# Dissolving the table stage of a decoder step into the gather stage that follows it

## What is computed

```
score = einsum(relu(qi . ki), wi)                 # cheap scores over all keys
_, idx = top_k(score, 256)                        # per sample: 256 of 4097 keys
k_sel, v_sel = cache[page_table[idx // 128], idx % 128]
logits = q . k_sel / 8 + rel_bias[t5_bucket(qpos - idx)]
p = softmax(where(valid, logits, -inf));  o = p . v_sel
merged = sigmoid(gate_a) * (att @ w_attn_out) + sigmoid(gate_s) * (ssd_y @ w_ssd_out)
```

## Time and profile before

| what | value |
| --- | --- |
| median of 3 runs | 4491.07 us (4490.77 to 4492.65) |
| the profiled execution | 4487.59 us |
| its span | 4485.8 us |
| PE, DVE, ACT, POOL busy | 91%, 41%, 16%, 5% of the span |
| mean granted clock of PE | 0.942 of full speed |
| table stage | 2677.1 to 2706.5 us of the span |
| gather stage | 2706.5 to 2879.1 us of the span |

### The profile page before, as it was taken

The page is one execution under the profiler, slowest core; times in us unless marked ns, Lnnn a source line. Parts: engine busy times, 40 slices in busy tenths (PEclk is TensorE's granted clock), DMA queues, the critical chain, the costliest instruction groups (busy, mean ns, idle before and its releaser), DMA issues. The chain is left out here.

```text
span 4485.8 us, 48370 instructions
## 1 busy us (share of the span) xinstructions
PE 4092.7 (91%) x17960; PEld 2927.2 (65%) x17960; DVE 1838.2 (41%) x3624; ACT 725.8 (16%) x1421; POOL 223.2 (5%) x224
## 2 busy tenths in 40 slices
PE   7999999989977978988988978899988989999997
PEld 5888776656655555665655645566656678888664
DVE  4222220010035676586586575257861143333001
ACT  2000000010021220211311300145611010000000
POOL 0000000000000020010100201200000100000000
PEclk9999999999957989999999988899998999999999
DMA  4121221114132101101001011320022111111111
GB/s 171 76 112 76 94 96 64 45 70 169 71 78 64 36 22 57 38 16 57 33 21 57 28 32 56 100 71 19 6 82 96 65 50 47 38 47 42 69 39 57
DMA packets 98898, 277.21 MB, mean 62 GB/s; under 512 B 18473, under 2 KB 54321, under 8 KB 87073
## 3 DMA queue, kind: packets, MB, share of 16 engines
q1 hardware_dynamic: 80464, 239.13, 15.5%
q0 software_dynamic: 3200, 21.11, 1.3%
q10 hardware_dynamic: 15072, 14.82, 1.1%
HBM read 228.18 MB, written 47.00 MB: 61 GB/s over the span
## 5 line engine op out<-in xcount | busy, mean ns | idle before, releaser
L1648 PE MATMUL banks<-h,arena 128*128 128x344 f32 x1920 | 586.6, 465 | 30.9 <-DMA arena<-in_w_ssd 30.9
L472 PE MATMUL f_ps<-f_a,f_w 128*128 128x344 f32 x2112 | 611.2, 452 | 1.9 <-issue 1.9
L472 PEld LDWEIGHTS f_ps<-f_a,f_w 128*128 128x128 f32 x2112 | 401.1, 190 | 211.3 <-issue 2.3
L1648 PEld LDWEIGHTS banks<-h,arena 128*128 128x128 f32 x1920 | 368.7, 195 | 232.9 <-DMA arena<-in_w_ssd 32.7
L363 PE MATMUL f_ps<-h,f_w 128*128 128x258 f32 x1408 | 327.7, 386 | 13.0 <-ACT h L209 12.1
L363 PE MATMUL f_ps<-room 128*128 128x258 f32 x1408 | 328.3, 393 | 2.5 <-issue 1.8
L363 PE MATMUL f_ps<-h,room 128*128 128x258 f32 x1408 | 320.9, 381 | 1.1 <-DVE f_u L633 1.0
L363 PEld LDWEIGHTS f_ps<-h,f_w 128*128 128x128 f32 x1408 | 269.7, 192 | 64.5 <-issue 23.6
L363 PEld LDWEIGHTS f_ps<-room 128*128 128x128 f32 x1408 | 275.1, 196 | 45.8 <-issue 2.7
L363 PEld LDWEIGHTS f_ps<-h,room 128*128 128x128 f32 x1408 | 266.9, 190 | 41.0 <-DVE f_u L633 1.9
L707 PE MATMUL banks<-y,arena 128*128 128x344 f32 x768 | 239.2, 474 | 38.2 <-DVE y L2058 30.1
(11 more groups left out here) (380 smaller groups left out, 4866.4 us busy)
## 6 DMA issues: line engine op xcount, KB each, us to landing
f_wa<-in_w_ada SPq DMA_DIRECT2D x28, 1024.0 KB
f_w<-in_w_f1i SPq DMA_DIRECT2D x22, 1024.0 KB, 4.7
f_w<-in_w_f2i SPq DMA_DIRECT2D x22, 1024.0 KB, 4.7
arena<-in_w_ssd SPq DMA_DIRECT2D x40, 512.0 KB, 3.6
f_w<-in_w_f1o SPq DMA_DIRECT2D x16, 704.0 KB, 4.1
f_w<-in_w_f2o SPq DMA_DIRECT2D x16, 704.0 KB, 4.1
room<-in_x SPq DMA_DIRECT2D x16, 516.0 KB, 7.7
scr_x<-room SPq DMA_DIRECT2D x16, 516.0 KB, 5.2
```

The costliest lines, as they stand in the source:

```text
L472: m = nc.tensor.matmul(ps[n][:, q, 0:NC], wo[:, hf, k], a[:, hf * OK + k, n * NC:(n + 1) * NC], start=hf == 0 and k == 0, stop=hf == 1 and ...
L1648: m = nc.tensor.matmul(ps[q][:, c, 0:NC], w[:, q, k], h[:, k, c * NC:(c + 1) * NC], start=k == 0, stop=k == KT - 1)
```

## The change

`tables` is removed as a stage, and its work is written into the streams of `gate_and_gather`:

- SP issues the three table loads first, then the first two gate tiles; then it waits for the subtraction, stores the tables, waits for the stores, issues the read-back, and goes on with the gate tiles (written out instead of looped). The table's buffers are cut out of `kvb`, which the gathers fill later.
- PE makes the table products first, into the banks of the later one-hot products. The three chunks of the first gate tile are set between the selection's products, and the eight flips between the second and the third gate tile, with a wait for the read-back ahead of them and a wait for all eight copies behind them. The loop is written out.
- DVE handles the table products ahead of the selection, and copies the flips between the mask's scaling and the first one-hots.
- POOL waits ahead of its first gather until the flips are done and the bias rows stored; its last wait, for the landed rows, is dropped. DVE waits for them before it reads the keys in `sample_attend_and_out`, PE before it reads the values. The index buffers therefore live on past the stage (`rows_at`).

```diff
-def tables(nc, d, s, bias):
-    ...
 def gate_and_gather(...)
+        at, up = carve(kvb, 0, [P, NH, WIN])
+        at, hot = carve(kvb, at, [NBUCKET, 512])
...
+        pf = [pE[n // 2][n % 2] for n in range(4)]
...
         def _(sp):
-            load_tiles(sp, w, w_in, gmm, NCH, d["w_gs"], KT)
+            sp.dma_start(hot, d["hot"]).then_inc(tabled, 16)
+            sp.dma_start(rb, d["rel_bias"]).then_inc(tabled, 16)
+            sp.dma_start(flip, d["flip"]).then_inc(tabled, 16)
+            for t in range(KT):
+                if t == 2:
+                    sp.wait_ge(sub, UP + 1)
+                    sp.dma_start(scr["byh"], byh).then_inc(b_stored, 16)
+                    sp.dma_start(scr["brow"].rearrange("(c p) h -> p c h", c=2), brow_t).then_inc(b_stored, 16)
+                    sp.wait_ge(b_stored, UP + 32)
+                    win = bass.AP(scr["byh"].tensor, 0, [[1, P], [512, NH], [1, WIN]])
+                    sp.dma_start(up, win).then_inc(b_back, 16)
+                if t >= 2:
+                    sp.wait_ge(gmm, UP + NCH * (t - 1))
+                sp.dma_start(w[:, t % 2], d["w_gs"][t]).then_inc(w_in[t % 2], 16)
...
         def _(pe):
+            pe.wait_ge(tabled, UP + 48)
+            nc.tensor.matmul(pf[0][0:NH, :], rb, hot, start=True, stop=True).then_inc(tabbed, 1)
+            for c in range(2):
+                nc.tensor.matmul(pf[1][:, c * NH:(c + 1) * NH], hot[:, c * P:(c + 1) * P], rb, ...).then_inc(tabbed, 1)
             pe.wait_ge(split, UP + 4)
...
+            chunk(0, 0)
             pe.wait_ge(chosen, UP + 1)
...
+            chunk(0, 1)
             pe.wait_ge(ranked, UP + 1)
...
-            gate(0, 0)
-            gate(0, 1)
+            chunk(0, 2)
+            gate(1)
+            pe.wait_ge(b_back, UP + 16)
+            pe.wait_ge(sub, UP + 1)
+            for n in range(NH // 2):
+                if n >= 4:
+                    pe.wait_ge(flipped, UP + n - 3)
+                nc.tensor.matmul(pf[n % 4][:], flip, up[:, 2 * n:2 * n + 2]...).then_inc(tabbed, 1)
             pe.wait_ge(valsd, UP + 1)
-            with pe.Fori(0, NB // 4) as i:
+            pe.wait_ge(flipped, UP + NH // 2)
+            for j in range(NB // 2):
+                gate(BEFORE + j)
...
         def _(dve):
+            dve.wait_ge(tabbed, UP + 3)
+            nc.vector.tensor_copy(byh, pf[0][0:NH, :]).then_inc(moved, 1)
+            nc.vector.tensor_copy(brow_t, pf[1][:, 0:2 * NH]...).then_inc(moved, 1)
+            dve.wait_ge(moved, UP + 2)
+            nc.vector.tensor_scalar(byh, byh, pf[0][0:NH, 0:1], None, ALU.subtract).then_inc(sub, 1)
...
+            for n in range(NH // 2):
+                dve.wait_ge(tabbed, UP + 4 + n)
+                nc.vector.tensor_copy(bias[:, 2 * n:2 * n + 2]..., pf[n % 4][:]).then_inc(flipped, 1)
...
         def _(pool):
+            pool.wait_ge(flipped, UP + NH // 2)
+            pool.wait_ge(b_stored, UP + 32)
...
-            pool.wait_ge(gathered, n)
...
 def sample_attend_and_out(...)
...
             pe.wait_ge(ptd, UP + 1)
+            pe.wait_ge(gathered, GATHERED)
...
             take(1)
+            dve.wait_ge(gathered, GATHERED)
```

More of the change, by code:

```diff
@@ L2128, in ssd_branch, with gate_and_gather @@
             ssd_out(nc, arena, banks, d, g, xc, zs, y, ones, dskip, nssd, S, mask)
-def gate_and_gather(nc, d, scr, h, S, mask, ident, pick, gathered, cnt, seln, kvb, brows, spare):
+def gate_and_gather(nc, d, scr, h, S, mask, ident, pick, gathered, cnt, seln, kvb, brows, rows_at, spare, bias):
     RING = 2 * NPAGE
@@ L2150, in gate_and_gather @@
         where = ph.sb("where", [P, 3, NB, 2])
-        row = ph.sb("row", [P, NB, 2], U32)
-        brow = ph.sb("brow", [P, NB, 2], U32)
+        row, brow = rows_at[:, 0], rows_at[:, 1]
+        at, up = carve(kvb, 0, [P, NH, WIN])
+        at, hot = carve(kvb, at, [NBUCKET, 512])
+        at, rb = carve(kvb, at, [NBUCKET, NH])
+        at, byh = carve(kvb, at, [NH, 512])
+        at, brow_t = carve(kvb, at, [P, 2, NH])
+        at, flip = carve(kvb, at, [P, P])
+        tabled, tabbed, moved, sub, b_stored, b_back, flipped = (
+            ph.sem(n) for n in ("tabled", "tabbed", "moved", "sub", "b_stored", "b_back", "flipped"))
         kv = kv_view(kvb)
@@ L2196, in _, with chunk, gate @@
         def _(pe):
-            def gate(i, q):
-                pe.wait_ge(w_in[q], UP + 16 * (i + 1))
-                for c in range(NCH):
[L2200 to L2205, removed]
+            def chunk(t, c):
+                q = t % 2
+                if c == 0:
+                    pe.wait_ge(w_in[q], UP + 16 * (t // 2 + 1))
+                if t:
+                    pe.wait_ge(gread, UP + NCH * (t - 1) + c + 1)
+                for k in range(KT):
+                    m = nc.tensor.matmul(ps[:, c, 0:NC], w[:, q, k], h[:, k, c * NC:(c + 1) * NC], start=k == 0, stop=k == KT - 1)
+                m.then_inc(gmm, 1)
+            def gate(t):
+                for c in range(NCH):
+                    chunk(t, c)
+            pe.wait_ge(tabled, UP + 48)
+            nc.tensor.matmul(pf[0][0:NH, :], rb, hot, start=True, stop=True).then_inc(tabbed, 1)
+            for c in range(2):
+                nc.tensor.matmul(pf[1][:, c * NH:(c + 1) * NH], hot[:, c * P:(c + 1) * P], rb, start=True, stop=True).then_inc(tabbed, 1)
             pe.wait_ge(split, UP + 4)
@@ L2602, in program @@
             kvb = buf(c2, "kvb", [P, 2 * (PAST + 1)])
[L2603 removed]
+            brows, rows_at = buf(c2, "brows", [P, NB, 2, NH]), buf(c2, "rows_at", [P, 2, NB, 2], U32)
             kT, qs = buf(c2, "kT", [P, 2, TOK]), buf(c2, "qs", [P, NH // 2, NB])
@@ L2606, in program @@
                 bias = buf(c3, "bias", [P, NH, WIN])
-                tables(nc, d, scr, bias)
-                gate_and_gather(nc, d, scr, h, S, mask, ident, pick, gathered, cnt, seln, kvb, brows, kT)
+                gate_and_gather(nc, d, scr, h, S, mask, ident, pick, gathered, cnt, seln, kvb, brows, rows_at, kT, bias)
                 attend(nc, d, scr, h, kT, qs, tok, mask, bias, ident, att)
-            sample_attend_and_out(nc, d, scr, kT, qs, tok, ones, ident, cnt, seln, kvb, brows, att, h, mask)
+            sample_attend_and_out(nc, d, scr, gathered, kT, qs, tok, ones, ident, cnt, seln, kvb, brows, att, h, mask)
         sums = buf(ctx, "sums", [P, 3, TOK])
```

32 lines of the change are left out of this document (17 added, 15 removed).

## The result

| | before | after |
| --- | --- | --- |
| median (4 runs each) | 4491.55 us (4490.77 to 4492.65) | 4447.11 us (4440.19 to 4451.94) |
| ratio, 95% interval | | 0.99 [0.9883, 0.9917] |
| profiled execution, its span | 4487.59, 4485.8 us | 4440.19, 4438.0 us |
| first table load to the load of kT for the prompt's attention | 201.95 us | 158.66 us |

What follows compares the result with a forecast made beforehand. TensorE bounds the gather stage once gate products run, with a chain of waits ahead. Saving 16.6 us there, minus 0.8 for stage ends, plus 0.4 for loops, gives 16.2: 4491.1 to 4474.9 us, range 4470 to 4483.

Steps and rivals of the forecast that it cites:

- The sum to the third gate tile: From the first table load's issue to the third gate tile: 50.8 us against 67.4, 16.6 us less.
- Table loads: Start of the stage: loads now share the queues with other loads and weight tiles, +1.0 us on their 2.82.
- Store and read-back, selection: Ahead of the third gate tile: 11.82 us of store and read-back, waits of 2.46 and 1.73, hidden under gate products.
- Flips: After the second gate tile: 9.0 us against 9.29 before, with two TensorE gaps of some 1.3 and 0.85 us.
- Clock at the flips: TensorE's gaps at the flips cost no clock: 0 charged, 1.7 us as the other bound.
- The clock rival: Clock falls at the small products between chunks, transposes and flips: 5.1 to 8.7 us, 4480.0 to 4483.6; chance 0.15.
- late loads: Table loads land late and hold the selection: 3.5 us more than charged, 4478.4; chance 0.10 together with uncovered selection.
- a late read-back: TensorE waits before the flips for the 2 MB read-back; slower if over 9 us, time then 4500; chance 0.04.
- an uncovered selection: Gate chunks fail to cover the selection's waits: 4.2 us come back, 4479.1; chance 0.10 together with late loads.
- Stage ends: The table stage's seven semaphores are now cleared at the gather stage's end: 0.8 us charged, bounds 0 and 1.0.
- Unrolled loops: TensorE's gate loop written out saves the 0.44 us gap at its turn: 0.4 credited, bounds -0.5 and 0.5.
- something unseen: Remainder for causes not listed anywhere in the forecast: chance 0.05, about half of it slower.

Runs made afterwards that it cites:

- loop_const_addr: Kernel before, TensorE's loop kept, but both turns read the first four samples' page and row numbers, so one-hot product addresses are constant: 4473.5 us, ratio 0.9961.
- register_addr: Changed kernel, gate tiles still written out, one-hot products in loops of two turns with a register in their address: 4472.79 us, ratio 0.9965.
- loop_ends_only: Changed kernel with a loop of one turn round each half group of one-hot products, all addresses constant: 4446.34 us, ratio 0.9901 to before.
- attention_written_out: Changed kernel with TensorE's loops in the prompt's attention written out too: 4447.43 us, ratio 0.9905 to before.
- mask_later: Changed kernel with VectorE's scaling of the mask moved behind the flips' copies: 4445.33 us, ratio 0.9903 to before.
- written_out_mask_later: Changed kernel with TensorE's prompt attention loops written out and the mask's scaling behind the flips' copies: 4453.16 us, ratio 0.9918 to before.

## Why the prediction was wrong

The table part was right, by its own steps.

- *The sum to the third gate tile*: 50.8, measured 50.31; selection's first product at t = 9.52, under the 12 that I set. That it is this close is partly luck: the loads (+0.2), the spread products (+0.3) and the flips (+0.4: 9.38 us from 2716.27 to 2725.65) took longer, the gate tiles (-0.5) and the two selection products between them (-0.7) less.
- *Table loads*: TensorE starts 4.02 us after the first issue (2679.36 - 2675.34), 1.2 more than before; I charged 1.0.
- *Store and read-back, selection*: both hidden. Without the chunks 5.8 us come back, where I had 4.2: the loads came 0.6 later in that run, and the lone products took 0.59 and 0.69 us, not 0.28 and 0.38; that is 1.2 of the 1.6 us between.
- *Flips*: two gaps, 1.25 and 0.83 (forecast 1.3 and 0.85); the eighth copy ends some 9 us after the second gate tile.
- *Clock at the flips*: 1.00 over the whole stretch (2716.20:2725.60 above). The Trainium skill's rule ("TensorE: Matmul & The Clock Gate", "A second HAM failure mode: psum-queue depth-cycling") was not borne out here, at gaps of 1.25 and 0.83 us. The clock rival fell with it; the others, late loads, a late read-back and an uncovered selection, did not come about.
- *Stage ends*: store of S to kT's load 9.79 us (2824.21 to 2834.00), before 9.03 (2870.04 to 2879.07): +0.76; I charged 0.8.
- *The wait for gathered rows*: 0, by an experiment of its own.

The step that failed is *Unrolled loops*: "I credit 0.4 (bounds -0.5 and 0.5 ...)". Its term is 27.0 us in the change and 24.1 alone; it came under "something unseen", which had 0.05. I took the loop's price to be its turn, and never asked what a loop does to the instructions inside it. The trace of before had the answer: 256 register operations at the line of the products, and products of three columns at 62 ns on the average, a rate that I read off nowhere, so that I had nothing to compare. It had no row for such a product without a register, so the term wanted far wider bounds than the turn gives. "From the third gate tile to the stage's end nothing should differ by more than 1.5 us" was the sentence by which the forecast could fall, and it did.

That 62 ns is also a figure of the Trainium skill ("TensorE: Matmul & The Clock Gate", section "Back-to-back issue gap"): what a small matmul costs when instructions are not decoded in hardware, against an issue floor of about 25 ns. The floor agrees with the 26 ns here. The 62 here is not such a price of each product: within a pair the second product starts 36 to 46 ns behind the first, and only the next pair waits; with the address alone made constant all come at 26 ns.

Shown, then: the products' rate comes from registers in their addresses (loop_const_addr, register_addr, loop_ends_only), 18.5 us, and the loop put back brings the whole 27 back. Not settled: what decides the clock behind groups of 3.4 us at 26 ns. It fell behind none in three traces of the change and one of attention_written_out, which has the change's code up to the attention, and behind one to four in one trace each of kernels that differ from it (mask_later one, loop_ends_only two, written_out_mask_later three, loop_const_addr all). Rows show two ends alone: behind groups of 6.6 us and more, at either rate, it always fell, behind halves of 1.76 us with no wait in them never. The 7.8 us of clock are therefore shown for the traced executions of this code, and without a cause that would carry over.

## What to carry to other kernels

Before pricing an unrolled loop, list the register operations inside it by line, with the operations that use their addresses: where these are short, a register in their address can set the rate, and the price is the difference in rate times the count, not the turn. Beside products of 277 ns and more, where 234 register operations stood in 401 us, the same unrolling gave 0.6 us at most. When one engine's piece becomes faster, look at once at what fed it: here the earlier one-hots, worth nothing before, were worth 1.25 us, or 3 if the clock behind the wait is theirs too.

## What the runs showed of the hardware

- Products of 128x128 by three f16 columns come every 26 ns with constant addresses. With a loop's register in an operand's address and one register operation of 55 ns for each pair, a pair takes 133 ns. TensorE's queue works ahead of the array: behind a gate tile some 27 products still came at 26 ns, so that a group of 128 has 62 on the average.
- The clock can fall without any idle time on TensorE: it was 0.50 for 4 us behind 256 products that came back to back (PE busy 6.50 of 6.50 us), as it was behind slow ones. It fell while they ran: 0.85 over the group.
- Clearing seven semaphores more at a stage's end took 0.76 us, 0.11 each: 20 clears from 2876.7 to 2878.7 us before, 27 from 2830.9 to 2833.6 in the change.
